# Gate matrices of a product-key expert layer: one float32 product per token in place of three bf16 products, with half of the weighting on ScalarE

## The chip, the cores and the metric

The kernel runs on one core of a Trainium2 chip. The metric is device time in microseconds (us) of one launch, as a median of several runs. TensorE (PE in the rows) multiplies matrices, VectorE (DVE) and ScalarE (ACT) work elementwise, GpSimd (POOL) here splits weights and issues gathers, and SyncE (SP) issues most transfers. PEld is the loading of the stationary operand into TensorE, which overlaps its matmuls.

## The reference

One decoder layer for 528 prompt tokens and 64 sample tokens: norm, one wide input projection, a short gated convolution, a chunked state-space scan, an output projection, and then PEER, a retrieval of single-neuron experts. The change touches PEER alone:

```
s = einsum(q, sub_keys)                       # per head: 2 x 128 scores
s_top, i_top = top_k(s, 16)                   # per half
best_s, best_c = top_k(all 16 x 16 sums, 16)
i1, i2 = the two half keys of each pick       # eid = i1 * 128 + i2
g = softmax(best_s)
act = gelu(u_tab[eid] . t)
out = sum over 8 heads x 16 picks of g * act * v_tab[eid]
```

Each token thus has 128 picks, each of them a pair of keys (i1, i2) with a weight g.

## The kernel before

For 448 of the 576 kept tokens the kernel doesn't gather the experts. It computes the activations of all 16,384 experts densely, multiplies them by a gate that is zero where a token didn't pick the expert, and multiplies by the second table densely too. For the other 128 tokens it gathers rows with indirect DMAs (L603, on POOL), and DVE makes a dot product with each (`row_dot`, L1877).

The dense part runs in 128 units. `activations(m)` on PE (the matmuls of L888) is 24 float32 matmuls of 448 columns, from weights that ACT copies into a rounded high part (`expert_hi`, L1298) and POOL completes with a low part (L611, `w_lo`, two slots). `gelu` (L1321) on ACT reads the result. The first 73 units run beside the search for the picks; `scores(j)` (L901) there is 16 plain float32 matmuls with 128 columns of keys as the moving operand, five sets of them.

Then come the gates, in NB = 28 blocks of TB = 16 tokens. The 128 picks of a token stand on the partitions. For a token, `oh_a` is a 128x128 one-hot matrix (pick x first key) and `oh_w` one of pick x second key times the weight; their product over the picks is the token's gate matrix, exactly as the sum over picks puts it. The operands are bf16. So that the float32 weight isn't rounded it is held as three bf16 pieces (`pickb[:, 2:5]`, made by L1967 to L1969 out of `wrest`), and each token takes three matmuls that add up in PSUM (L937), 48 per block.

- DVE, `one_hots(b, par)`: two comparisons (L1959, L1960) and three multiplications (L1963 twice, L1964), each of 128x2048 bf16, into one of two buffer pairs. It may start when `gates(b - 2)` is done (s_gm) and ends with s_oh.
- PE, `gates(b, par, first)`: waits for s_oh and for the copy of the block before (s_gt), then the matmuls into PSUM banks 4 to 7.
- ACT, `gates_out(b)` (L1363): copies the banks to `gt`, from where SP stores to DRAM.

The order on each engine is written out by hand. PE runs the gates of a block and then `UB[b]` units: one unit in 12 of the 28 blocks, two in the other 16. A block with one unit is called short here. DVE runs the one-hots of block b + 1 and then the dot products of block b (two, or three in every fourth block). After the gates the kernel finishes the units, loads gates and activations back, and runs the second table.

Of the kernel before, what the change touches and what calls it, by code (L numbers as in the profile page):

```python
# [5 lines left out]
ALU = mybir.AluOpType  # L6
ACT = mybir.ActivationFunctionType
# [132 lines left out]
def trunk(nc, xT, x_rows, units, keys, cols, heads, hist_a, hist_s, ssm_in, rows_u, rows_v,  # L140
# [6 lines left out]
    with ExitStack() as ctx:  # L147
        def at(name, off, shape, dt=F32):
            n = 2 if dt is BF16 else 4
# [11 lines left out]
        def stack(start):  # L161

            pos = [start]

            def put(name, shape, dt=F32):
                n = 2 if dt is BF16 else 4
# [9 lines left out]
        ident = const("ident", [P, P])  # L176
        A_CAUSAL = pos[0]
        causal = const("causal", [P, P])
# [121 lines left out]
        mid, mpos = stack(R_MA)  # L300
        pickb = mid("pickb", [P, 5, ND], BF16)
        wrest = mid("wrest", [P, ND])
        iota2 = at("iota2", A_CAUSAL, [P, P, 2], BF16)
        ge = [mid(f"ge{i}", [P, ND]) for i in range(2)]
# [6 lines left out]

        oh_a = at("oh_a", R_XS, [P, 2, TW_, P, 2], BF16)
        oh_w = at("oh_w", R_XS + 4 * TB * P, [P, 2, 3, TW_, P, 2], BF16)
        gt = at("gt", R1, [P, 2, NKEYS, SB])
# [115 lines left out]
        s_eq = sem("one_hots_compared")  # L430
        s_oh = sem("one_hots_ready")
        s_gm = sem("gates_built")
        s_gt = sem("gates_copied")
# [186 lines left out]
        def _(pe):  # L620
# [309 lines left out]
            def gates(b, par, first):  # L930
                pe.wait_ge(s_oh, b + 1)
                if not first:
                    pe.wait_ge(s_gt, b)
                for j in range(TB):
                    a, c = divmod(j, 2)
                    for i in range(3):
                        last = mm(ps[:, 4 + j // 4, j % 4 * P:(j % 4 + 1) * P], oh_a[:, par, a, :, c],  # L937
                                  oh_w[:, par, i, a, :, c], start=i == 0, stop=i == 2)
                last.then_inc(s_gm, 1)
# [45 lines left out]
        def _(act):  # L985
# [353 lines left out]
            for j in range(len(TT)):  # L1339
# [9 lines left out]
                if j:  # L1349
                    act.wait_ge(s_pkT, j)  # L1350
                    n = P if heads == PH else HALF
                    here = slice(TT[j][0], TT[j][0] + n)
                    act.activation(pickb[:, 0:3, here], S0[:, 0:3 * P].rearrange("p (a t) -> p a t", a=3)[:, :, 0:n],
                                   ACT.Copy)
                    act.activation(wrest[:, here], S0[:, 2 * P:2 * P + n], ACT.Copy).then_inc(s_pks, 1)


            def gates_out(b):
                B, part_ = b // 2, b % 2
                act.wait_ge(s_gm, b + 1)  # L1360
                if B >= 2 and part_ == 0:
# [3 lines left out]
                               ACT.Copy).then_inc(s_gt, 1)  # L1365

            activated(M_TOP)
            activated(M_TOP + 1)
            for b in range(NB):
                gates_out(b)  # L1370
                for m in range(M_BLOCK[b], M_BLOCK[b + 1]):
                    activated(m)
# [79 lines left out]
        def _(dve):  # L1452
# [436 lines left out]
            for j, (t0, heads) in enumerate(TT):  # L1889
# [28 lines left out]
                if j == 0:  # L1918
                    dve.tensor_copy(steps[:], iota[:, 0:TOPK])
                    dve.tensor_copy(iota2[:], iota[:].unsqueeze(2).to_broadcast([P, P, 2]))  # L1920
                link(dve.tensor_copy(bself[:, :, 0:np_], bsel[:, :, 0:np_]))
# [28 lines left out]
            def one_hots(b, par):  # L1950
                if b >= 2:
                    dve.wait_ge(s_gm, b - 1)
                t0 = b * TB
                shape = [P, TW_, P, 2]
                across = iota2[:].unsqueeze(1).to_broadcast(shape)
                key_a, key_b, *weight = (pickb[:, i, t0:t0 + TB].rearrange("p (a c) -> p a c", c=2).unsqueeze(2)
                                         .to_broadcast(shape) for i in range(5))
                plain = oh_w[:, par, 2]
                tt_(plain, across, key_b, ALU.is_equal).then_inc(s_eq, 1)  # L1959
                tt_(oh_a[:, par], across, key_a, ALU.is_equal)  # L1960
                dve.wait_ge(s_eq, b + 1)
                for i in range(2):
                    tt_(oh_w[:, par, i], plain, weight[i], ALU.mult)  # L1963
                tt_(plain, plain, weight[2], ALU.mult).then_inc(s_oh, 1)  # L1964

            dve.wait_ge(s_pks, len(TT) - 1)
            link(tt_(wrest[:], wrest[:], pickb[:, 2], ALU.subtract))  # L1967
            link(dve.tensor_copy(pickb[:, 3], wrest[:]))
            link(tt_(pickb[:, 4], wrest[:], pickb[:, 3], ALU.subtract))  # L1969
            one_hots(0, 0)  # L1970
# [160 lines left out]
```

## Time and profile before

| | us |
|---|---|
| median of 3 runs | 2379.86 (2379.05 to 2383.71) |
| the profiled execution | 2379.05 |
| its span, first to last instruction | 2377.1 |
| PE busy in the span | 2344.5 (99%) |
| DVE busy | 1614.3 (68%) |
| POOL busy | 1412.2 (59%) |
| ACT busy | 772.7 (33%) |

The execution's own time is 1.95 us above its span. A matmul in plain float32 with 128 columns leaves two records in the trace, so the 16 matmuls of a set of scores read x32. A row of the timeline gives start, duration, engine, line, operation, output <- inputs, and in brackets how long the engine sat idle before it and who released it. Durations of successive instructions overlap by about a tenth of a us on ACT and DVE and by more on PE, so paces are read from starts.

### The profile page before, as it was taken

The numbers are of one execution on the slowest core, as the hardware profiler recorded it, in microseconds if no ns is written. First come the engines' busy times: TensorE is split into PE (matmuls) and PEld (weight loads), VectorE is DVE, ScalarE is ACT, GpSimd is POOL, SyncE is SP. The second block draws the span as 40 slices with busy tenths as digits, with TensorE's granted clock in tenths as the row PEclk, the third lists the DMA queues.
The fourth block names the chain that finished last, engine by engine and source line by source line (L and its number), as shares of the span: only waits on it lengthen the run. The fifth ranks groups of instructions, "written<-read, shape, count | busy, mean of one in ns | idle before, by whom it ended". The sixth has DMA issues, their size and how long they took to land.

```text
span 2377.1 us, 38840 instructions
## 1 busy us (share of the span) xinstructions
PE 2344.5 (99%) x14998; PEld 2188.6 (92%) x14998; DVE 1614.3 (68%) x2671; ACT 772.7 (33%) x1059; POOL 1412.2 (59%) x787
## 2 busy tenths in 40 slices
PE   9999999999999999999999999999999999999998
PEld 9999999987899999999999989999889999999997
DVE  7865444556775244097987879999577766677774
ACT  4432323332231012233343344444333333333332
POOL 5554334432444555447676757777667777777763
PEclk9999999999999999999999999999999999999999
DMA  5223223236742232247676759999988888888872
GB/s 215 77 80 140 93 99 97 98 108 229 270 171 83 81 128 95 86 134 268 236 261 238 251 169 329 327 329 319 352 302 325 322 315 333 317 319 318 324 269 76
DMA packets 207745, 510.05 MB, mean 215 GB/s; under 512 B 15857, under 2 KB 104305, under 8 KB 205169
## 3 DMA queue, kind: packets, MB, share of 16 engines
q1 hardware_dynamic: 115552, 236.75, 30.9%
q10 hardware_dynamic: 55184, 137.07, 15.5%
q0 software_dynamic: 36864, 134.23, 15.2%
q8 instruction: 100, 1.64, 0.3%
q14 instruction: 45, 0.36, 0.0%
HBM read 424.55 MB, written 83.44 MB: 214 GB/s over the span
## 4 chain that ended last, share of the span: by engine, by line
PE 91%; DVE 5%; DMA 2%; ACT 1%; issue 1%; ACTq 0%; DVEq 0%; SPq 0%; POOL 0%; POOLq 0%
PE ps L888 51%; PE ps L635 30%; PE ps L937 3%; DVE prev L1678 1%; PE ps L901 1%; PE ps L807 1%; PE ps L794 1%; PE ps L802 1%; PE ps L811 1%; DMA gbuf<-gate_scratch 1%; PE ps L827 1%; DMA cxb<-parked_tiles 0%; PE ps L660 0%; PE ps L780 0%; DMA raw<-units 0%
## 5 line engine op out<-in xcount | busy, mean ns | idle before, releaser
L584 POOL TENSOR_SCALAR w_hi<-raw 128x1024 fp32r<-128x1024 f32 x129 | 139.2, 1079 | 521.1 <-issue 391.6
L611 POOL TENSOR_TENSOR w_lo<-raw,e_hi 128x1024 fp32r<-128x1024 f32 x128 | 320.7, 2505 | 176.6 <-PE ps L888 169.1
L611 POOL TENSOR_TENSOR w_lo<-raw,w_hi 128x1024 fp32r<-128x1024 f32 x128 | 315.8, 2468 | 180.7 <-PE ps L888 179.5
L888 PE MATMUL ps<-p_hi,w_lo 128*128 128x448 f32 x1024 | 375.0, 366 | 0.0
L888 PE MATMUL ps<-g_hi,w_lo 128*128 128x448 f32 x1024 | 374.7, 366 | 0.0
L586 POOL TENSOR_TENSOR w_lo<-raw,w_hi 128x1024 fp32r<-128x1024 f32 x129 | 319.1, 2473 | 10.7
L635 PE MATMUL ps<-h_hi,w_hi 128*128 128x296 f32 (+1 forms) x1216 | 273.7, 306 | 1.8 <-ACT ma L1204 1.8
L635 PE MATMUL ps<-h_lo,w_hi 128*128 128x296 f32 (+1 forms) x1216 | 262.5, 297 | 0.0
L635 PE MATMUL ps<-h_hi,w_lo 128*128 128x296 f32 (+1 forms) x1216 | 262.2, 297 | 0.0
L1298 ACT ACTIVATE e_hi<-raw 128x1024 fp32r<-128x1024 f32 x128 | 135.8, 1061 | 263.2 <-DMA raw<-units 126.4
L635 PEld LDWEIGHTS ps<-h_hi,w_hi 128*128 128x128 f32 x1216 | 196.1, 188 | 25.9 <-issue 23.8
L888 PEld LDWEIGHTS ps<-g_hi,w_lo 128*128 128x128 f32 x1024 | 192.2, 188 | 15.1
L888 PEld LDWEIGHTS ps<-p_hi,w_lo 128*128 128x128 f32 x1024 | 192.2, 188 | 15.1
L1298 ACT ACTIVATE w_hi<-raw 128x1024 fp32r<-128x1024 f32 x128 | 135.9, 1062 | 197.4 <-PE ps L888 156.2
L635 PEld LDWEIGHTS ps<-h_lo,w_hi 128*128 128x128 f32 x1216 | 196.2, 188 | 0.0
L635 PEld LDWEIGHTS ps<-h_hi,w_lo 128*128 128x128 f32 x1216 | 196.1, 188 | 0.0
L888 PE MATMUL ps<-g_hi,w_hi 128*128 128x448 f32 x512 | 188.6, 368 | 1.3 <-ACT abuf L1319 1.3
L603 POOL DMA_INDIRECT ug<-rows_u,eid x128 | 170.3, 1331 | 30.8 <-issue 16.7
L888 PE MATMUL ps<-p_hi,e_hi 128*128 128x448 f32 x512 | 186.7, 365 | 1.8 <-DVE p_lo L2006 1.6
L888 PE MATMUL ps<-g_hi,e_hi 128*128 128x448 f32 x512 | 188.2, 368 | 0.2 <-ACT abuf L1319 0.2
L888 PE MATMUL ps<-p_hi,w_hi 128*128 128x448 f32 x512 | 187.2, 366 | 0.2 <-DVEq L1987 0.2
L888 PE MATMUL ps<-p_lo,w_hi 128*128 128x448 f32 x512 | 187.1, 365 | 0.0
(337 smaller groups left out, 5176.9 us busy)
## 6 DMA issues: line engine op xcount, KB each, us to landing
raw<-units SPq DMA_DIRECT2D x385, 512.0 KB
gate_scratch<-gt SPq DMA_DIRECT2D x56, 512.0 KB
activation_scratch<-ge ACTq DMA_DIRECT2D x120, 224.0 KB
abuf<-activation_scratch ACTq DMA_DIRECT2D x30, 896.0 KB, 6.1
gbuf<-gate_scratch ACTq DMA_DIRECT2D x30, 896.0 KB
prev<-ssm_in ACTq DMA_DIRECT2D x8, 1024.0 KB, 7.0
ssm_s<-prev ACTq DMA_DIRECT2D x8, 1024.0 KB, 4.2
parked_tiles<-stage ACTq DMA_DIRECT2D x24, 296.0 KB, 2.1
```

The costliest lines, as they stand in the source:

```text
L584: pool.tensor_scalar(w_hi[:, s, :], raw[:, r, :], 1.0, 1.0, ALU.mult, ALU.mult).then_inc(s_whi, 1)
L586: pool.tensor_tensor(w_lo[:, s, :], raw[:, r, :], w_hi[:, s, :].bitcast(F32), ALU.subtract)\
L603: pool.indirect_dma_start(out=ug[j % UG][:], out_offset=None, in_=table, in_offset=bass.IndirectOffsetOnAxis(ap=eid[:, k:k + 1], axis=0)). ...
L611: pool.tensor_tensor(w_lo[:, n % 2, :], raw[:, n % RAW, :], e_hi[m % HS_].bitcast(F32), ALU.subtract)\
L635: last = mm(a[:, h, :], w, m[:, k0 + k, t0 + h * w_:t0 + (h + 1) * w_], start=start and k == 0 and i == 0, stop=stop and k == KT - 1 and i ...
L794: mm(S1[p0:p0 + HEADDIM, h // 2 * n:(h // 2 + 1) * n], xh, wT[0:n, h, 0:n], start=True, stop=True)
L802: last = mm(S2[j % 2 * n:(j % 2 + 1) * n, :], cmf[:, b * TS:(b + 1) * TS], prev[:, (2 * g + j // 4) % 3, j % 4, :], start=j < 2, stop=j >= ...
L807: last = mm(S2[:, j * n:(j + 1) * n], state[:, g, j * P:(j + 1) * P], Cg, start=True, stop=True)
L811: mm(S3, bT[0:n, :], xde[0:n, :], start=True, stop=True).then_inc(s_st, 1)
L888: last = mm(accp[par], w[:, k * P:(k + 1) * P], x_[:, k, t0:t0 + ND], start=k == 0 and i == 0, stop=k == KT - 1 and i == 2)
L937: last = mm(ps[:, 4 + j // 4, j % 4 * P:(j % 4 + 1) * P], oh_a[:, par, a, :, c], oh_w[:, par, i, a, :, c], start=i == 0, stop=i == 2)
L1298: act.activation(e_hi[m % HS_], raw[:, n % RAW, :], ACT.Copy).then_inc(s_ehi, 1)
```

## The change

The one-hots are float32, and each token takes one plain float32 matmul in place of three bf16 ones. The weight is no longer cut in pieces. It is multiplied into the first-key one-hot, `oh_g`; the second, `oh_2`, stays plain. DVE multiplies the first 8 tokens of a block (`TW_`), and ACT the other 8 in a new helper `weigh`, one activation of 128x128 each with the weight as a scale per partition, in place. PE waits for the new semaphore s_ow besides s_oh. The interleaved copy of the counting row (`iota2`) goes, and `pickb` and `wrest` become one tile `pickT`.

```diff
@@ tiles
-        pickb = mid("pickb", [P, 5, ND], BF16)
-        wrest = mid("wrest", [P, ND])
-        iota2 = at("iota2", A_CAUSAL, [P, P, 2], BF16)
+        pickT = mid("pickT", [P, 3, ND])
-        oh_a = at("oh_a", R_XS, [P, 2, TW_, P, 2], BF16)
-        oh_w = at("oh_w", R_XS + 4 * TB * P, [P, 2, 3, TW_, P, 2], BF16)
+        oh_g = at("oh_g", R_XS, [P, 2, TB, P])
+        oh_2 = at("oh_2", R_XS + 8 * TB * P, [P, 2, TB, P])
@@ PE, gates
                 pe.wait_ge(s_oh, b + 1)
+                pe.wait_ge(s_ow, b + 1)
                 if not first:
                     pe.wait_ge(s_gt, b)
                 for j in range(TB):
-                    a, c = divmod(j, 2)
-                    for i in range(3):
-                        last = mm(ps[:, 4 + j // 4, j % 4 * P:(j % 4 + 1) * P], oh_a[:, par, a, :, c],
-                                  oh_w[:, par, i, a, :, c], start=i == 0, stop=i == 2)
+                    last = mm(ps[:, 4 + j // 4, j % 4 * P:(j % 4 + 1) * P], oh_g[:, par, j, :], oh_2[:, par, j, :],
+                              start=True, stop=True)
@@ ACT
-                    act.activation(pickb[:, 0:3, here], S0[:, 0:3 * P].rearrange("p (a t) -> p a t", a=3)[:, :, 0:n],
-                                   ACT.Copy)
-                    act.activation(wrest[:, here], S0[:, 2 * P:2 * P + n], ACT.Copy).then_inc(s_pks, 1)
+                    act.activation(pickT[:, :, TT[j][0]:TT[j][0] + n],
+                                   S0[:, 0:3 * P].rearrange("p (a t) -> p a t", a=3)[:, :, 0:n],
+                                   ACT.Copy).then_inc(s_pks, 1)
+            def weigh(b):
+
+                act.wait_ge(s_eq, b + 1)
+                for j in range(TW_, TB):
+                    oh = oh_g[:, b % 2, j, :]
+                    t = b * TB + j
+                    last = act.activation(oh, oh, ACT.Copy, scale=pickT[:, 2, t:t + 1])
+                last.then_inc(s_ow, 1)
+
             activated(M_TOP)
+            act.wait_ge(s_pks, len(TT) - 1)
+            weigh(0)
             activated(M_TOP + 1)
             for b in range(NB):
                 gates_out(b)
+                if b + 1 < NB:
+                    weigh(b + 1)
                 for m in range(M_BLOCK[b], M_BLOCK[b + 1]):
                     activated(m)
@@ DVE, one_hots
-                plain = oh_w[:, par, 2]
-                tt_(plain, across, key_b, ALU.is_equal).then_inc(s_eq, 1)
-                tt_(oh_a[:, par], across, key_a, ALU.is_equal)
+                across = iota[:].unsqueeze(1).to_broadcast([P, TB, P])
+                key_a, key_b, weight = (pickT[:, i, t0:t0 + TB].unsqueeze(2).to_broadcast([P, TB, P]) for i in range(3))
+                tt_(oh_g[:, par], across, key_a, ALU.is_equal).then_inc(s_eq, 1)
+                tt_(oh_2[:, par], across, key_b, ALU.is_equal)
                 dve.wait_ge(s_eq, b + 1)
-                for i in range(2):
-                    tt_(oh_w[:, par, i], plain, weight[i], ALU.mult)
-                tt_(plain, plain, weight[2], ALU.mult).then_inc(s_oh, 1)
+                low = oh_g[:, par, 0:TW_]
+                tt_(low, low, weight[:, 0:TW_], ALU.mult).then_inc(s_oh, 1)
             dve.wait_ge(s_pks, len(TT) - 1)
-            link(tt_(wrest[:], wrest[:], pickb[:, 2], ALU.subtract))
-            link(dve.tensor_copy(pickb[:, 3], wrest[:]))
-            link(tt_(pickb[:, 4], wrest[:], pickb[:, 3], ALU.subtract))
             one_hots(0, 0)
```

On PE, at the second block of gates, the kernel before has this row of instructions (acc0_read: the accumulator is free; weights_split: the low part of the weights is there):

```order
L888 MATMUL ps<-g_hi,w_lo 128x448
L937 MATMUL ps<-oh_w,oh_a 128x128 [waits gates_copied,one_hots_ready]
L937 MATMUL ps<-oh_w,oh_a 128x128 x47
L888 MATMUL ps<-g_hi,e_hi_156 128x448 [waits acc0_read,weights_split]
L888 MATMUL ps<-g_lo,e_hi_156 128x448
```

The changed kernel has there (oh_174 is oh_2 under a number of the allocator; its lines are numbered anew):

```order
L886 MATMUL ps<-g_hi,w_lo 128x448
L934 MATMUL ps<-oh_174,oh_g 128x128 [waits gates_copied,one_hots_weighted,one_hots_ready]
L934 MATMUL ps<-oh_174,oh_g 128x128 x15
L886 MATMUL ps<-g_hi,e_hi_163 128x448 [waits acc0_read,weights_split]
L886 MATMUL ps<-g_lo,e_hi_163 128x448
```

The burst stands at the same place, with 16 matmuls for 48, and waits for one more semaphore. On ACT, from the last copy of picks to the gates of the first block, before:

```order
L1353 ACTIVATE pickb<-ps 128x3x64
L1355 ACTIVATE wrest<-ps 128x64
L1321 ACTIVATE ge_164<-ps 128x448
L1323 DMA activation_scratch<-ge_164 128x448
L1298 ACTIVATE e_hi_165<-raw 128x1024
L1321 ACTIVATE ge_163<-ps 128x448
L1323 DMA activation_scratch<-ge_163 128x448
L1298 ACTIVATE w_hi<-raw 128x1024
L1363 ACTIVATE gt<-ps 128x128x16
```

And in the changed kernel:

```order
L1349 ACTIVATE pickT<-ps 128x3x64
L1318 ACTIVATE ge_162<-ps 128x448
L1320 DMA activation_scratch<-ge_162 128x448
L1295 ACTIVATE e_hi_163<-raw 128x1024
L1369 ACTIVATE oh_g<-oh_g,pickT 128x128 x8
L1318 ACTIVATE ge_161<-ps 128x448
L1320 DMA activation_scratch<-ge_161 128x448
L1295 ACTIVATE w_hi<-raw 128x1024
L1359 ACTIVATE gt<-ps 128x128x16
L1369 ACTIVATE oh_g<-oh_g,pickT 128x128 x8
```

Eight activations come between two units ahead of the first gates, and eight behind each copy of gates, ahead of the next unit's gelu.

## Rows read from the trace of the kernel before

**Rows 1.** The page: busy time, share of the span, instructions.
```profile
PE 2344.5 (99%) x14998; PEld 2188.6 (92%) x14998; DVE 1614.3 (68%) x2671; ACT 772.7 (33%) x1059; POOL 1412.2 (59%) x787
```

**Rows 2.** Two windows: length, busy per engine, PEclk, DMA share, GB/s.
```profile
1400.00:1690.00 290.00, 290.00 (x2353) 269.38 (x2352) 273.27 (x257) 121.24 (x115) 207.66 (x102) 1.00 0.94 311
...
1394.50:1397.50 3.00, 2.95 (x29) 2.98 (x30) 3.00 (x3) 0.00 (x0) 0.00 (x0) 0.52 0.44 164
```

**Rows 3.** Chain of waits around the gates: start, us, what.
```profile
1391.12 3.30 DVE oh_w L1964
...
1394.55 4.22 PE ps L937 x48
...
1663.81 4.92 PE ps L888 x24
1668.73 2.77 PE ps L937 x48
1671.50 9.78 PE ps L888 x48
```

**Rows 4.** Waits from 1380 to 1690: total us, times, longest.
```profile
DVE ug L1877 <- DMA ug<-rows_u,eid: 14.9, 13, 4.1
...
ACT gt L1363 <- DMA gate_scratch<-gt: 6.1, 3, 3.0
PE ps L937 <- DVE oh_w L1964: 4.2, 1, 4.2
```

**Rows 5.** Chain of waits at two sets of scores.
```profile
1084.86 3.57 PE ps L901 x32
...
1259.03 3.26 PE ps L901 x32
```

**Rows 6.** Timeline of PE at a set of scores.
```profile
1084.70 3.73 PE L901 MATMUL ps<-key_sb,q 128*128 128x128 f32 x32
1088.18 0.45 PE L888 MATMUL ps<-g_hi,w_hi 128*128 128x448 f32 x1
```

**Rows 7.** Timeline of PE at a block of gates.
```profile
1501.86 2.93 PE L937 MATMUL ps<-oh_w,oh_a 128*128 128x128 bf16 x48
1504.60 0.45 PE L888 MATMUL ps<-g_hi,w_hi 128*128 128x448 f32 x1
```

**Rows 8.** Timeline of ACT: before the first gates, after a later block, and early.
```profile
1386.61 1.06 ACT L1298 ACTIVATE e_hi<-raw 128x1024 fp32r<-128x1024 f32 x1 [0.47 <-ACT ge L1321]
...
1504.83 1.88 ACT L1363 ACTIVATE gt<-ps 128x2048 f32<-128x2048 f32 x1 [0.63 <-PE ps L937]
...
9.80 3.50 ACT L1019 ACTIVATE hu_hi<-x,col 128x592 fp32r<-128x592 f32 x5
```

**Rows 9.** ACT by line and shape: count, busy, mean ns, idle before.
```profile
L1298 ACT ACTIVATE e_hi<-raw 128x1024 fp32r<-128x1024 f32 x128 | 135.8, 1061 | 263.2 <-DMA raw<-units 126.4 <-PE ps L888 102.4 <-ACT ge L1321 26.6
L1394 ACT ACTIVATE p_hi<-abuf 128x448 fp32r<-128x448 f32 x128 | 72.5, 567 | 30.2 <-DVE abuf L2001 23.6 <-issue 6.3
...
L1019 ACT ACTIVATE hu_hi<-x,col 128x592 fp32r<-128x592 f32 x8 | 5.6, 779 | 0.0
```

**Rows 10.** Timeline of DVE: before the first gates, and around block 26.
```profile
1382.53 0.62 DVE L1967 TENSOR_TENSOR wrest<-wrest,pickb 128x448 f32<-128x448 f32 x1 [7.77 <-ACT wrest L1355]
...
1663.83 3.43 DVE L1963 TENSOR_TENSOR oh_w<-oh_w,pickb 128x2048 bf16<-128x2048 bf16 x1
1667.18 1.21 DVE L1964 TENSOR_TENSOR oh_w<-oh_w,pickb 128x2048 bf16<-128x2048 bf16 x1
```

**Rows 11.** One DVE line: ns min/median/max, starts, forms.
```profile
L1650 DVE TENSOR_TENSOR seg<-ps,dqT x20: 682/1225/1226, 236.7 to 589.0; 128x1024 f32<-128x1024 f32 x16, 64x512 f32<-64x512 f32 x4
```

**Rows 12.** POOL by line, 1380 to 1690: count, busy, mean ns, idle before.
```profile
L603 POOL DMA_INDIRECT ug<-rows_u,eid x58 | 97.8, 1686 | 13.6 <-issue 10.4 <-DVE dots L1877 0.5 <-PE ps L888 0.3
L611 POOL TENSOR_TENSOR w_lo<-raw,w_hi 128x1024 fp32r<-128x1024 f32 x24 | 60.8, 2535 | 39.7 <-PE ps L888 39.5
```

**Rows 13.** The gathers' line over the whole span: ns min/median/max, starts.
```profile
L603 POOL DMA_INDIRECT ug<-rows_u,eid x128: 937/962/1972, 1077.9 to 1723.1; - x128
```

More of the change, by code:

```diff
@@ L148, in at @@
         def at(name, off, shape, dt=F32):
-            n = 2 if dt is BF16 else 4
+            n = 4
             for s in shape[1:]:
@@ L165, in put @@
             def put(name, shape, dt=F32):
-                n = 2 if dt is BF16 else 4
+                n = 4
                 for s in shape[1:]:
@@ L176, in trunk @@
         ident = const("ident", [P, P])
-        A_CAUSAL = pos[0]
         causal = const("causal", [P, P])
@@ L431, in trunk @@
         s_oh = sem("one_hots_ready")
+        s_ow = sem("one_hots_weighted")
         s_gm = sem("gates_built")
@@ L1351, in _ @@
                     n = P if heads == PH else HALF
-                    here = slice(TT[j][0], TT[j][0] + n)
-                    act.activation(pickb[:, 0:3, here], S0[:, 0:3 * P].rearrange("p (a t) -> p a t", a=3)[:, :, 0:n],
-                                   ACT.Copy)
-                    act.activation(wrest[:, here], S0[:, 2 * P:2 * P + n], ACT.Copy).then_inc(s_pks, 1)
+                    act.activation(pickT[:, :, TT[j][0]:TT[j][0] + n],
+                                   S0[:, 0:3 * P].rearrange("p (a t) -> p a t", a=3)[:, :, 0:n],
+                                   ACT.Copy).then_inc(s_pks, 1)
             def gates_out(b):
@@ L1919, in _ @@
                     dve.tensor_copy(steps[:], iota[:, 0:TOPK])
-                    dve.tensor_copy(iota2[:], iota[:].unsqueeze(2).to_broadcast([P, P, 2]))
                 link(dve.tensor_copy(bself[:, :, 0:np_], bsel[:, :, 0:np_]))
@@ L1953, in one_hots @@
                 t0 = b * TB
[L1954 to L1957, printed above, removed]
-                plain = oh_w[:, par, 2]
-                tt_(plain, across, key_b, ALU.is_equal).then_inc(s_eq, 1)
-                tt_(oh_a[:, par], across, key_a, ALU.is_equal)
+                across = iota[:].unsqueeze(1).to_broadcast([P, TB, P])
+                key_a, key_b, weight = (pickT[:, i, t0:t0 + TB].unsqueeze(2).to_broadcast([P, TB, P]) for i in range(3))
+                tt_(oh_g[:, par], across, key_a, ALU.is_equal).then_inc(s_eq, 1)
+                tt_(oh_2[:, par], across, key_b, ALU.is_equal)
                 dve.wait_ge(s_eq, b + 1)
-                for i in range(2):
-                    tt_(oh_w[:, par, i], plain, weight[i], ALU.mult)
-                tt_(plain, plain, weight[2], ALU.mult).then_inc(s_oh, 1)
+                low = oh_g[:, par, 0:TW_]
+                tt_(low, low, weight[:, 0:TW_], ALU.mult).then_inc(s_oh, 1)
             dve.wait_ge(s_pks, len(TT) - 1)
-            link(tt_(wrest[:], wrest[:], pickb[:, 2], ALU.subtract))
-            link(dve.tensor_copy(pickb[:, 3], wrest[:]))
-            link(tt_(pickb[:, 4], wrest[:], pickb[:, 3], ALU.subtract))
             one_hots(0, 0)
```

## The prediction

> **What bounds the kernel now.** I read the page's busy times first, then the windows of the gate stage, the chain of waits through it, the table of waits, and last the timelines of single engines. PE is busy for 99% of the span [rows 1]. In the stage that the change touches, 1400 to 1690 us, it is busy for all 290 us at the full clock, while DVE is busy for 273 of them (94%), POOL for 208 and ACT for 121 [rows 2]. The chain there is PE alone: a burst of gates of 2.77 us, 4.92 us for one unit or 9.78 us for two, and so on [rows 3]. So each us that a burst grows is a us on the end, as long as nobody else is late. Two things are to be seen besides. PE waits in this stage in earnest just once: 4.2 us for DVE's last one-hot before the first burst [rows 4]. And that first burst takes 4.22 us instead of 2.77 [rows 3]; the granted clock in its first 3 us is 0.52 [rows 2], the lower of the two levels (1.2 instead of 2.4 GHz), which it fell to behind that wait. And DVE, though off the chain, has little to spare: in block 26, a short one, its last product ends at 1668.39 (1667.18 + 1.21 [rows 10]) and the burst starts at 1668.73 [rows 3], 0.34 us later.
>
> **The burst on PE.** Removed per block: 48 bf16 matmuls. Added: 16 plain float32 matmuls of 128x128 by 128 columns. That is exactly a set of scores, L901: same shape, same banks, each followed by a unit. Its price is in the trace twice over. By the chain, 3.57 us [rows 5] against 2.77 [rows 3], 0.80 more. From starts, burst to first unit matmul behind it: 1088.18 - 1084.70 = 3.48 us [rows 6] against 1504.60 - 1501.86 = 2.74 [rows 7], 0.74 more. The one set with 64 tokens (half the stationary width) takes 3.26 [rows 5], 0.49 more; I keep that as the low end although its shape differs. With 28 blocks: 28 x 0.74 = 20.7, 28 x 0.80 = 22.4, low end 28 x 0.49 = 13.7. I take 21.0, near the count from starts, since starts are recorded and ends modelled. A third as many matmul instructions is thus not a third of the time: a float32 matmul costs 3.48/16 = 218 ns and a bf16 one 2.74/48 = 57 ns, so one replaces three of 171 ns in all. Nothing hides the difference, PE being the chain.
>
> **The first block.** Three vector operations (L1967 to L1969) go, and the one-hots can begin at 1382.5, where L1967 starts now [rows 10]. PE would have been ready at 1394.55 - 4.2 = 1390.35 [rows 3, 4]. DVE: float32 products took 625 ns for 448 columns (0.62 [rows 10]) and 1225 ns for 1024 [rows 11], so 1.04 ns a column, and 2.29 us for 2048, 1.22 for the 1024 of the multiplication; spaced 0.1 closer each, 5.5 us in all, ending at 1388.0, or at 1390.3 if POOL's split (2.5 us [rows 12]) holds up one of them as in block 26, where a product of 1.21 took 3.43 [rows 10], 2.2 us more. ACT: it ends e_hi at 1386.61 + 1.06 = 1387.67 [rows 8] and then weighs. Price of one weighing: no activation of 128 columns with a scale per partition stands in the rows. From 1061 ns for 1024 columns and 567 for 448 a column costs 0.86 ns; the one with such a scale has 779 ns for 592 [rows 9], so 779 - 464 x 0.86 = 380 ns for 128. Five in a row of those took 3.50 us [rows 8], (3.50 - 0.78)/4 = 0.68 apart, 0.1 closer than their duration. So 0.28 us each, between 0.2 (a further tenth of overlap) and 0.38 (none). I take 0.28, by the row that has the same kind of scale: 2.24 us, ending at 1389.9; at 0.38, 1390.7. All three arrive at about 1390.3. The wait of 4.2 us goes but for some tenths, and the clock doesn't fall, so the burst gives back 4.22 - 2.77 = 1.45 too: 5.65, of which I count 5.4.
>
> **The later blocks, ACT.** The new wait of PE is for ACT. What is queued behind the weighing there is the next gelu, the next store and e_hi; gelu frees the accumulator for the unit after next, at least 4.9 us on. The tight case is a short block. The copy starts at 1504.83 and takes 1.88 [rows 8], the weighing 2.24, so it ends at 1508.95. PE's next burst would start at 1504.60 + 4.92 + 0.2 = 1509.7. The slack of 0.76 us is used up at 0.375 us each, so even the high end loses 0.04 us in each of 12 blocks, 0.5 in all. Copies that wait for stores (3, 6.1 us in all [rows 4]) come, by their starts, ahead of two-unit stretches, where twice the slack is there. I count nothing.
>
> **The later blocks, DVE.** Five products of 1.21 us spaced 1.13 apart, 5.65 us, become 2.2 + 2.2 + 1.1 = 5.5. The wait for the first comparison is met one instruction later. ACT needs the first comparison only, which comes 2.2 us after the start; the bounds for DVE are a gain of 0.15 us a block and one more stoppage by POOL, a loss of 2.2. Since each block of PE grows by 0.75 us and DVE's work doesn't, its slack should grow from block to block. Counted at nothing. Had it no slack left, a us of DVE in a short block would be a us of the end.
>
> **POOL.** A gather takes 0.96 us as a median over the span with a maximum of 1.97 [rows 13], but 1.69 as a mean in this stage [rows 12], where DVE runs products out of two SBUF tiles for half of the time. It ends up waiting for the DVE instruction under way. That instruction now lasts 2.3 us and not 1.2, so a gather may take up to 1.1 us more, and so may a split. POOL has 290 - 208 = 82 us idle [rows 2]; if each of the 58 gathers and twice 24 splits [rows 12] lost 0.55 us, 58 us would go, and it still keeps up. The Trainium skill, page SBUF — State Buffer, section Who interferes with whom, says that a vector instruction with two SBUF inputs contends with GpSimd instructions that read SBUF and not with those that only write, whoever issued first holding the port to the end. For the splits the trace agrees (3.43 for 1.21 [rows 10]); by that rule the gathers, which write descriptors, would be free of it, and their 1.69 against 0.96 speaks against that part. The sum by either is the same as long as POOL keeps up.
>
> **The sum.** 2379.05 + 21.0 - 5.4 = 2394.65 us for the execution profiled; that one is 0.8 below the median of the three. I say 2395.
>
> **The rivals.**
> 1. *A wait takes the place of the one removed.* DVE or POOL falls behind in short blocks: the stage has DVE at 94% [rows 2], slack of 0.34 us at block 26, and DVE already waits 14.9 us for gathered rows [rows 4]; with gathers held longer, rows land later, dot products come later, one-hots behind them too. Against it: PE's stage grows by 21 us and DVE's own work doesn't. If PE waits 1 us in each of the 12 short blocks, 2394.7 + 12 = 2407; at 2 us, 2419.
> 2. *The other side: faster.* The two records of a float32 matmul might run as one pass here, the one-hots being contiguous: 16 x 0.109 = 1.74 us a burst, 28 x (1.74 - 2.77) = -28.8, and 2345 with the 5.4. The place is the burst, and it decides below 2.74/16 = 171 ns a matmul, or below 183 with the first wait counted in (5.4/28/16 = 12 ns more). For it: one instruction in place of three. Against it: five sets of scores, out of contiguous tiles too, at 204 to 223 ns.
> 3. *Cheaper bursts.* At the low end of 0.49 us: 2379.05 + 13.7 - 5.4 = 2387.4. For it only the narrow set of scores.
> 4. *The first wait stays.* If ACT's eight activations or DVE's last product come 2 us late, 2 of the 4.2 stay and the clock may fall again: 2394.7 + 3.5 = 2398. It lies inside the range.
>
> **Chances.** Forecast with rival 4: 0.74, 2391 to 2400. Rival 1: 0.17. Rival 3: 0.05. Rival 2: 0.04. The range of 2388 to 2406 leaves out rival 2, most of rival 3's low part and the larger half of rival 1. A measurement of this kernel can tell 0.2% (4.8 us) from no change. Slower by more than that (from 2384.7 on): forecast, rival 1 and most of rival 3, 0.93. Within it: 0.03, from rival 3 and a milder rival 2. Faster: 0.04.
>
> **What would show it.** Per burst two records for each of 16 matmuls, and 3.5 to 3.6 us of the chain; the first burst near 1390.4 with no fall of the clock; no wait of PE for ACT's weighing or for DVE beyond some tenths; the eight weighings in 2.0 to 2.6 us; DVE comparisons of 2.3 us, some of 4.5; gathers up to 3 us long. The forecast is wrong if a burst takes less than 3.2 us, or if the table of waits has PE behind DVE, ACT or POOL in the short blocks with more than 5 us in all.

## The result, and the profile after

The changed kernel takes 2410.5 us as a median of 4 runs (2405.44 to 2411.7; seven further executions on record lie between 2407.87 and 2416.41), the kernel before beside it 2381.38 (2379.05 to 2383.71): a ratio of 1.0127, with a 95% interval of 1.0111 to 1.0142. It is slower, as forecast, but by 29 us and not by 16, and 2410.5 lies above the range. The profiled execution took 2407.87 us with a span of 2406.0, 28.9 above the span of before.

The busy times of the page, to be read beside [rows 1]:

```profile
PE 2380.0 (99%) x14550; PEld 2214.3 (92%) x14550; DVE 1607.6 (67%) x2611; ACT 837.2 (35%) x1279; POOL 1432.2 (60%) x787
```

The chain of waits of the changed kernel from 1383 on, which answers to [rows 3] (a burst is the row of matmuls that makes a block's gates, L934; L886 are the units):

```profile
1383.24 10.06 PE ps L886 x48
1393.30 3.62 PE ps L934 x32
1396.92 9.77 PE ps L886 x48
...
1423.70 4.87 PE ps L886 x24
1428.57 3.57 PE ps L934 x32
...
1700.27 3.57 PE ps L934 x32
1703.85 14.65 PE ps L886 x72
```

A burst is 3.57 us, to the hundredth what a set of scores costs [rows 5], and the first one 3.62, with no wait ahead of it. The timeline around the burst at 1428, to be read beside [rows 6, 7]: 1431.89 - 1428.40 = 3.49 us from start to start.

```profile
1428.40 3.73 PE L934 MATMUL ps<-oh,oh_g 128*128 128x128 f32 x32
1431.89 0.45 PE L886 MATMUL ps<-g_hi,e_hi 128*128 128x448 f32 x1
```

PE's own waits, over the whole span, the three longest. None is for a one-hot or a weighing, where [rows 4] has 4.2 us:

```profile
PE ps L706 <- POOL rowmask L573: 3.6, 1, 3.6
PE ps L825 <- DVE xs L1707: 2.7, 4, 0.7
PE ps L633 <- DVE hu_lo L1516: 2.0, 2, 1.6
```

With that the stage of the gates can be summed. From the start of the first burst to the end of the last it lasts 1703.85 - 1393.30 = 310.55 us, where the chain of before gives 1684.04 - 1394.55 = 289.49:

```profile
1681.28 2.77 PE ps L937 x48
1684.04 6.14 PE ps L888 x30
```

That is 21.06 more, 28 bursts against 28 bursts. But the ends lie further apart. Here is the whole account, from the chains and from the start of the first dense unit (1008.08 before, 1006.88 after):

| stretch | before | after | difference |
|---|---|---|---|
| to the first dense unit | 1008.08 | 1006.88 | -1.2 |
| dense units until PE is ready for the first burst | 382.27 | 386.42 | +4.15 |
| wait for the one-hots | 4.20 | 0 | -4.2 |
| first burst to end of last burst | 289.49 | 310.55 | +21.06 |
| from there to the end of the span | 693.06 | 702.15 | +9.1 |
| span | 2377.1 | 2406.0 | +28.9 |

Two stretches grew, 4.15 and 9.1 us, in which no matmul was changed, and one of them lies ahead of the first burst. What they have in common is the dense unit. In the same 300 us of the second table, so many of its matmuls start; the first row is the kernel before, the second the changed one (two separate answers, with the length, PE's busy time and count, the clock, DMA share and GB/s):

```profile
1960.00:2260.00 300.00, 299.91 (x1480) 1.00 0.88 322
```

```profile
1960.00:2260.00 300.00, 300.00 (x1460) 1.00 0.87 317
```

1480 against 1460, 202.7 ns against 205.5, at full clock and with PE busy throughout. The matmuls of the projections before 1003 us kept their pace (2896 start between 200 and 600 us in both kernels). 6144 matmuls of a dense unit stand in the span, so 2 to 3 ns on each is the whole of what the sum lacked (28.9 - 15.6 = 13.3 us, or 2.2 ns each).

### The profile page after: what moved, and what is told of

Its sections match the earlier page's. It is cut to its first block, busy times and chain, and to the rows that moved or that the text cites. A ratio compares the mean times of both kernels' runs of the same rounds, so it can differ in the third digit from the quotient of the medians.

```text
span 2406.0 us, 38105 instructions
## 1 busy us (share of the span) xinstructions
PE 2380.0 (99%) x14550; PEld 2214.3 (92%) x14550; DVE 1607.6 (67%) x2611; ACT 837.2 (35%) x1279; POOL 1432.2 (60%) x787
## 4 chain that ended last, share of the span: by engine, by line
PE 91%; DVE 5%; DMA 2%; ACT 1%; issue 1%; DVEq 0%; SPq 0%; ACTq 0%
PE ps L886 52%; PE ps L633 29%; PE ps L934 4%; DMA cxb<-parked_tiles 1%; DVE prev L1687 1%; PE ps L899 1%; PE ps L805 1%; PE ps L792 1%; PE ps L800 1%; PE ps L809 1%; PE ps L825 1%; PE ps L658 0%; DMA gbuf<-gate_scratch 0%; PE ps L778 0%; DVE hu_lo L1516 0%
## 5 line engine op out<-in xcount | busy, mean ns | idle before, releaser
L609 POOL TENSOR_TENSOR w_lo<-raw,w_hi 128x1024 fp32r<-128x1024 f32 x128 | 324.3, 2534 | 188.3 <-PE ps L886 187.5
L886 PE MATMUL ps<-p_hi,w_lo 128*128 128x448 f32 x1024 | 376.2, 367 | 0.0
L886 PE MATMUL ps<-g_hi,w_lo 128*128 128x448 f32 x1024 | 375.6, 367 | 0.0
L584 POOL TENSOR_TENSOR w_lo<-raw,w_hi 128x1024 fp32r<-128x1024 f32 x129 | 318.5, 2469 | 10.8
L886 PEld LDWEIGHTS ps<-p_hi,w_lo 128*128 128x128 f32 x1024 | 192.2, 188 | 18.2
L886 PEld LDWEIGHTS ps<-g_hi,w_lo 128*128 128x128 f32 x1024 | 192.2, 188 | 17.5
L1886 DVE CUSTOM_DVE_ANT_0 ug<-ug,ps 128x1024 f32<-128x1024 f32 x128 | 153.7, 1213 | 78.3 <-DMA ug<-rows_u,eid 78.0
L601 POOL DMA_INDIRECT ug<-rows_u,eid x128 | 179.2, 1400 | 29.2 <-issue 17.9
L1986 DVE TENSOR_TENSOR x<-x,ps 128x448 f32<-128x448 f32 x128 | 79.5, 621 | 167.8 <-PE ps L886 164.6
L886 PE MATMUL ps<-g_hi,w_hi 128*128 128x448 f32 x512 | 189.5, 370 | 1.4 <-ACT abuf L1316 1.4
L886 PE MATMUL ps<-p_hi,e_hi 128*128 128x448 f32 x512 | 187.5, 366 | 1.7 <-DVE p_lo L2007 1.6
L886 PE MATMUL ps<-g_hi,e_hi 128*128 128x448 f32 x512 | 188.9, 369 | 0.0
```

What stands on the lines that cost most here:

```text
L584: pool.tensor_tensor(w_lo[:, s, :], raw[:, r, :], w_hi[:, s, :].bitcast(F32), ALU.subtract)\
L601: pool.indirect_dma_start(out=ug[j % UG][:], out_offset=None, in_=table, in_offset=bass.IndirectOffsetOnAxis(ap=eid[:, k:k + 1], axis=0)). ...
L609: pool.tensor_tensor(w_lo[:, n % 2, :], raw[:, n % RAW, :], e_hi[m % HS_].bitcast(F32), ALU.subtract)\
L886: last = mm(accp[par], w[:, k * P:(k + 1) * P], x_[:, k, t0:t0 + ND], start=k == 0 and i == 0, stop=k == KT - 1 and i == 2)
L1886: dve.tensor_tensor_reduce(rows, rows, h_rows, 1.0, 0.0, ALU.mult, ALU.add, dots[:, k:k + 1])\
L1986: tt_(xu, xu, accp[p_], ALU.add).then_inc(s_x2, 1)
```

## The experiments

Every time is a median beside runs of the kernel before on the same chip; that kernel's own median was 2382.03, 2382.6, 2381.44 and 2384.0 in the four groups of runs.

**Where the units' pace comes from.** The change also altered a placement: `pickT` is 896 bytes smaller than `pickb` and `wrest` together, and all tiles behind it in that stack moved down by that: the gelu buffers `ge`, `e_hi1` (one of the four slots of the weights' high part; e_hi0, w_hi[1] and w_hi[0] are the others), `eid` and a buffer for gathered rows. The first two runs exchange the placements.

```diff
+++ e1_layout_of_before (on the changed kernel)
         pickT = mid("pickT", [P, 3, ND])
+        mid("pad", [P, 224])
```

> The changed kernel with an unused tile of 896 bytes behind pickT, so that the tiles behind it (the two gelu buffers ge, e_hi1, eid, the last gathered-row buffer) stand at the addresses that they have in the kernel before. Theory P (place): the pace of the dense units, 205.5 ns a matmul in the changed kernel's second-table stage against 202.8 before, comes from where e_hi1 or the gelu buffers stand; then it returns to about 202.8, and the time to 2410.5 - 14 = 2396 (2393 to 2399), which is the sum of the prediction. Rival S (a state that doesn't hang on places, such as one that differs from one build or load to the next): the pace stays at 205 to 206 and the time within 3 us of 2410.

2397.41 us (2397.24 to 2399.57), ratio 1.0062 (1.0038 to 1.0086), and 1480 matmuls in the 300 us again:

```profile
1960.00:2260.00 300.00, 299.91 (x1480) 1.00 0.89 320
```

Its chain around the first burst, and from the last burst on:

```profile
1384.03 9.87 PE ps L887 x48
1393.90 0.00 issue
1393.90 3.81 PE ps L935 x32
...
1699.71 3.57 PE ps L935 x32
1703.28 14.65 PE ps L887 x72
```

Summed like the table above (first dense unit at 1011.69, span 2395.3), e1 has 382.21 us until the first burst, with no wait, 309.38 in the stage of the gates and 692.02 behind it. The two stretches outside the gates are back to what the kernel before has (382.27 and 693.06). In the stage e1 is 19.89 us above the kernel before, so 1.2 of the 21.06 us were the units' pace too. The span is 3.6 us longer for a reason that has nothing to do with the change: the first dense unit starts later. Over the 17 traces it starts anywhere between 1006.9 and 1014.6 us, so an account by stages says more than the spans of two single executions do.

```diff
+++ e2_before_moved (on the kernel before)
-        wrest = mid("wrest", [P, ND])
+        mid("pad", [P, 224])
-        eid = mid("eid", [P, N_PICK], U32)
+        eid = at("eid", A_CAUSAL + 512, [P, N_PICK], U32)
         ug = [...] + [mid(f"ug{UG - 1}", [P, D])]
+        wrest = mid("wrest", [P, ND])
```

> The kernel before with ge and e_hi1 moved 896 bytes down, to the addresses of the changed kernel (wrest goes behind them, eid onto constants no longer used, the last row buffer ends up 1408 bytes lower). Bf16 gates as before. Theory P: the pace of the dense units goes from 202.8 to about 205.5 ns, 6144 matmuls by 2.5 ns, so 2381 + 14 = 2395 (2391 to 2399). Rival S: 2381 within 3 us.

2395.86 us (2394.67 to 2399.94), ratio 1.0052 (1.0033 to 1.007), and the pace of the changed kernel under the instructions of before:

```profile
1960.00:2260.00 300.00, 300.00 (x1460) 1.00 0.88 316
```

Theory P holds both ways; S is out. Then which tile:

```diff
+++ e5_e_hi1_up (on the changed kernel)
+        mid("pad", [P, 224])
         e_hi1 = mid("e_hi1", [P, D], F32R)
+++ e6_behind_e_hi1 (on the changed kernel)
         e_hi1 = mid("e_hi1", [P, D], F32R)
+        mid("pad", [P, 224])
```

> The changed kernel with 896 unused bytes ahead of e_hi1: the gelu buffers stay where the change put them, and e_hi1, eid and the last row buffer stand as in the kernel before. Theory W (it is the place of the weights): the pace in the second-table stage goes from 205.7 to 202.8 ns, 487 matmuls in 100 us become 494, and the time is 2396. Rival G (the gelu buffers' place): 487 in 100 us and 2410.

> The changed kernel with the 896 unused bytes behind e_hi1: gelu buffers and e_hi1 as the change put them, eid and the last row buffer as before. Theory W: 487 matmuls in 100 us and 2410, as in the changed kernel. Rival R (the place of the gathered rows' buffer, which DMAs write): 494 and 2396.

e5: 2399.22 (2396.89 to 2399.98). e6: 2413.01 (two runs, 2407.41 and 2418.61). The windows, e5 first:

```profile
1960.00:2260.00 300.00, 299.91 (x1480) 1.00 0.88 321
```

```profile
1960.00:2260.00 300.00, 300.00 (x1460) 1.00 0.87 316
```

Neither the gelu buffers nor the row buffer matters to the pace. It is the place of e_hi1, a tile that the change doesn't name.

```diff
+++ e7_e_hi1_by_32 (on the changed kernel)
+        mid("pad", [P, 8])
         e_hi1 = mid("e_hi1", [P, D], F32R)
+++ e8_both_by_32 (as e7, and)
+        late("pad0", [P, 8])
         e_hi0 = late("e_hi0", [P, D], F32R)
```

> The changed kernel with 32 unused bytes ahead of e_hi1, which then starts at a multiple of 64 bytes, like the slots in w_hi and unlike e_hi0 (odd multiples of 32 in both kernels). Theory A (the alignment to 64 bytes sets the pace of a slot): units out of e_hi1 run at the pace that units of w_hi have, and the time moves from 2410 to between 2396 and 2405. Rival F (finer or coarser places count, not the multiple of 64): e_hi1's units stay at about 205 ns, 2410.

> The changed kernel with both e_hi0 and e_hi1 moved 32 bytes up, so that all four slots of the high parts start at multiples of 64 bytes. Theory A: one pace for all units, at the 202.8 of w_hi before (2396) or at the 206.7 that w_hi has in the changed kernel (about 2420). Rival F: as in the run with e_hi1 alone.

e7: 2402.79 (2399.46 to 2404.73). e8: 2397.36 (2393.09 to 2404.68). Both moved the time, so 32 bytes suffice, but neither theory had all of it. The pace in the second table, from the starts of successive matmuls within a unit, by the slot of its high part (ns a matmul). The residue is that of the slot's offset from the start of the kernel's own tiles; that start is itself at 128 modulo 256 in the partition, so the addresses in the partition have residues 128 further on. The expectations count as the table does:

| kernel | e_hi0 (mod 256) | e_hi1 (mod 256) | w_hi[1] (64) | w_hi[0] (64) |
|---|---|---|---|---|
| before | 204.3 (224) | 200.6 (160) | 202.9 | 203.1 |
| changed | 204.1 (224) | 204.9 (32) | 206.7 | 206.7 |
| e2 | 204.1 (224) | 204.9 (32) | 206.7 | 206.7 |
| e1, e5 | 204.3 (224) | 200.6 (160) | 202.8 | 202.9 |
| e7 | 204.4 (224) | 202.8 (64) | 202.8 | 202.6 |
| e8 | 201.1 (0) | 204.3 (64) | 204.2 | 204.1 |
| e9 | 201.3 (0) | 200.7 (160) | 202.9 | 203.1 |
| e14 | 201.2 (0) | 200.5 (160) | 202.8 | 202.9 |
| e15 | 204.0 (224) | 204.3 (224) | 202.8 | 202.8 |

Units out of w_hi, which never moved, run at 202.9 or 206.7 according to where e_hi1 is. The slots take turns in this order, so e_hi1's place reaches the two units behind it and not e_hi0's, which comes third (204.3 and 204.1). By what route it does is not shown; all slots share the low parts `w_lo` and the moving operand, and no run moved those.

```diff
+++ e9_before_e_hi0_up (on the kernel before)
+        late("pad0", [P, 8])
         e_hi0 = late("e_hi0", [P, D], F32R)
```

> The kernel before with e_hi0 32 bytes up (a multiple of 64), nothing else. In the run with both moved, units out of e_hi0 took 201.1 ns a matmul and not 204.3. If that belongs to e_hi0's own place, 1536 of the 6144 matmuls gain 3.2 ns: 5 us, 2377 against 2382, and 494 matmuls in 100 us become 497. Rival: the pace of a slot hangs on the pair of places and carries over into the next units; then the units of e_hi1 or w_hi lose what e_hi0 gains, 2382 or up to 2390.

2378.41 (2376.73 to 2383.14, 10 runs) against 2381.44: ratio 0.999 with an interval of 0.9978 to 1.0002, so the time alone doesn't settle it. The pace does: e_hi0's units 204.3 to 201.3, the others as before, and 1485 matmuls in the window.

```profile
1960.00:2260.00 300.00, 299.88 (x1485) 1.00 0.89 322
```

```diff
+++ e14_changed_both_places (on e5)
+        late("pad0", [P, 8])
         e_hi0 = late("e_hi0", [P, D], F32R)
+++ e15_before_e_hi1_by_64 (on the kernel before)
+        mid("pad", [P, 16])
         e_hi1 = mid("e_hi1", [P, D], F32R)
```

> The changed kernel with e_hi1 at its place of before (896 bytes up; 2399.2 alone) and e_hi0 32 bytes up. Theory: places act one by one, e_hi0's units at 201.3 and e_hi1's at 200.6 as in the kernel before with the same places; 2392 to 2395. Rival: in the changed kernel with e_hi1 32 bytes up, e_hi0's move slowed the three other slots by 1.4 ns each, and it does so here.

> The kernel before with e_hi1 64 bytes up, which puts it at 224 modulo 256, where e_hi0 stands in the kernel before (204.3 ns), instead of 160 (200.6). Theory M (the place modulo 256 sets a slot's own pace): e_hi1's units go to about 204.3 and the time to 2387 or more. Rival N: they stay at 200.6 to 201 and 2381, so that the place modulo 256 doesn't tell the pace.

e14: 2399.62 (2394.79 to 2404.81) where 2392 to 2395 was expected. The paces are those of the theory (201.2, 200.5, and w_hi untouched), and the median doesn't show it. The execution traced is the slowest of the three, and PE waits longer in it for the low part of the second table's moving operand, `p_lo`. The first row is e5, the second e14:

```profile
PE ps L887 <- DVE p_lo L2008: 1.6, 1, 1.6
```

```profile
PE ps L888 <- DVE p_lo L2009: 8.6, 3, 3.8
```

Eight of the 17 traces have such a further wait of 3.0 to 3.9 us (e14 has two), with and without the change, so part of the scatter of the times is likely this and not the place of a tile. What makes DVE late there stays open. e15: 2387.81 (2385.97 to 2392.8), ratio 1.0023 (1.0005 to 1.004), and e_hi1 at 204.3: theory M called it. Rival N is out for this place. The residue of 64 has given 202.8 and 204.3 though (e_hi1 in e7 and e8), so the residue modulo 256 alone doesn't tell a pace, and what the hardware does there stays open.

**What a burst is worth.**

```diff
+++ e3_two_pieces (on the kernel before)
-                    for i in range(3):
+                    for i in range(2):
                         ... start=i == 0, stop=i == 1)
```

> The kernel before with two of the three bf16 pieces of the weight multiplied in: 32 matmuls a block instead of 48 (the lowest piece of the weight is left out of the gates). All else, DVE's five products too, unchanged. Theory: a burst is on the path with its whole length, at 57 ns a matmul, so it takes 2.77 - 16 x 0.057 = 1.86 us in the chain and the time falls by 28 x 0.91 = 25 us to 2356; the pace of the units stays at 202.8. Rival: DVE, busy for 94% of the stage and with 0.3 us of slack in short blocks, becomes late as PE gets ahead; PE then waits for L1964 in the short blocks, and less than 15 of the 25 us come through (over 2366).

2384.41 (2375.21 to 2391.27, 8 runs), ratio 1.0006 (0.9988 to 1.0024): nothing came through, and the rival was right. The chain and the waits of that kernel:

```profile
1409.84 1.85 PE ps L937 x32
...
1423.27 4.92 PE ps L888 x24
1428.33 3.01 POOL w_lo L611
1431.49 8.09 DMA ug<-rows_u,eid
1439.60 1.22 DVE ug L1877
```

```profile
PE ps L937 <- DVE oh_w L1964: 24.7, 7, 5.1
```

The burst did fall to 1.85, as expected, and the chain leaves PE: it runs over POOL, the gather and DVE, and PE waits 24.7 us for the one-hots. The waits cost more than their length: behind the five of 4.0 us and more the burst took 2.7 to 3.4 us from its start to the next unit's, where the others took 1.8. The clock shows why, here behind the wait of 5.1 us:

```profile
1505.84:1508.84 3.00, 3.00 (x30) 3.00 (x31) 3.00 (x5) 0.00 (x0) 0.88 (x1) 0.52 0.96 307
```

The stage of before has two bounds that nearly touch. Then DVE's load was cut with PE's:

```diff
+++ e12_two_pieces_four_products (on e3)
-                plain = oh_w[:, par, 2]
+                plain = oh_w[:, par, 1]
-                for i in range(2):
-                    tt_(oh_w[:, par, i], plain, weight[i], ALU.mult)
-                tt_(plain, plain, weight[2], ALU.mult).then_inc(s_oh, 1)
+                tt_(oh_w[:, par, 0], plain, weight[0], ALU.mult)
+                tt_(plain, plain, weight[1], ALU.mult).then_inc(s_oh, 1)
-            link(tt_(pickb[:, 4], wrest[:], pickb[:, 3], ALU.subtract))
```

> The kernel before with two of the three bf16 pieces (the lowest is left out of the gates), and now DVE's third product for it left out too. With 32 matmuls and five products the bursts fell to 1.85 us, 25 us less, and nothing of it came through: PE waited 24.7 us for DVE. Theory: a shorter burst is worth its length only as far as DVE keeps up; with four products (1.1 us less in each of 28 blocks) the wait is mostly gone and 20 to 25 us come through: 2357 to 2362. Rival: something else holds the stage (gathered rows, POOL), 2375 or more.

2353.9 (2353.17 to 2359.88), ratio 0.9892 (0.9873 to 0.991). 27.5 us came through, above the expected 20 to 25. What was left out of the expectation is the first burst: with a product less, DVE is on time there too, the wait of 4.2 us shrinks to 0.2 and the clock stays up. What is left of PE's waits for the one-hots is 1.2 us in four waits, the longest 0.4. This version beats both kernels. With the better place for e_hi0 on top:

```diff
+++ e13_two_pieces_e_hi0_up (on e12)
+        late("pad0", [P, 8])
         e_hi0 = late("e_hi0", [P, D], F32R)
```

> The kernel before with two bf16 pieces, four products on DVE, and e_hi0 32 bytes up. Two pieces alone gave 2353.9; the move alone brought e_hi0's units from 204.3 to 201.3 ns a matmul, 1536 by 3 ns. Theory: the two add up, 2349. Rival: the pace gained at a place doesn't outlast another order of instructions, 2354.

2348.05 (2343.86 to 2357.79), ratio 0.986 (0.9828 to 0.9893); the paces are 201.1, 200.5, 202.8 and 202.9. The two gains add up, as far as a median of four with this scatter can tell. It is the fastest kernel tried, 36 us below the kernel before beside it and 62 below the changed one's own median. Both versions leave out the third piece, so their gates carry the weight to two bf16 pieces and not three.

**The first burst's wait.**

```diff
+++ e4_late_first (on the changed kernel)
+                if b == 0:
+                    for _ in range(2):
+                        link(tt_(oh_2[:, par], across, key_b, ALU.is_equal))
                 tt_(oh_g[:, par], across, key_a, ALU.is_equal).then_inc(s_eq, 1)
```

> The changed kernel with two more comparisons of 2.3 us ahead of the first block's on DVE (they write oh_2, which is then written anew), so that the first burst comes late again. Theory (the first-block term of the sum): DVE ends about 4.5 us later, PE waits some 4 to 4.6 us, the clock falls to the lower level for about 3 us and the first burst takes some 1.5 to 2.5 us more; 5.5 to 7 us more than the changed kernel in the stage. Rival: the clock stays up after a wait of that length, and only the wait itself is lost, 4 to 4.6.

2421.99 (two runs, 2421.02 and 2422.96) against 2410.5. Its wait, its first burst, and the clock in the first 3 us of it:

```profile
PE ps L934 <- DVE oh_g L1971: 6.5, 1, 6.5
```

```profile
1399.77 6.05 PE ps L934 x32
```

```profile
1399.77:1402.77 3.00, 3.00 (x14) 3.00 (x15) 3.00 (x2) 0.00 (x0) 0.00 (x0) 0.50 0.16 62
```

The wait came out at 6.5 us, not 4.5, since two of the comparisons took 4.4 us each beside POOL, and the product behind them was 2.2 us shorter. Behind it the clock is at the lower level (1.2 GHz) and the burst takes 6.05 instead of 3.62, 2.4 us more. 6.5 + 2.4 = 8.9 us against 5.5 to 7 expected (3.0 more of the 11.5 us is one of the waits for p_lo named above); the mechanism is the expected one, and the rival (the clock stays up) is out. In the changed kernel, without the wait, the same window reads 1.00.

```profile
1393.30:1396.30 3.00, 3.00 (x29) 3.00 (x28) 3.00 (x2) 1.60 (x2) 2.85 (x1) 1.00 0.58 225
```

**Who has slack beside the burst.** Both of these stand on e1, whose time is 2397.41.

```diff
+++ e10_act_weighs_12
-                for j in range(TW_, TB):
+                for j in range(TB - 12, TB):
-                low = oh_g[:, par, 0:TW_]
-                tt_(low, low, weight[:, 0:TW_], ALU.mult).then_inc(s_oh, 1)
+                low = oh_g[:, par, 0:TB - 12]
+                tt_(low, low, weight[:, 0:TB - 12], ALU.mult).then_inc(s_oh, 1)
+++ e11_dve_weighs_all
-                tt_(low, low, weight[:, 0:TW_], ALU.mult).then_inc(s_oh, 1)
+                tt_(oh_g[:, par], oh_g[:, par], weight, ALU.mult).then_inc(s_oh, 1)
                 (and weigh, its calls and PE's wait for s_ow removed)
```

> The changed kernel with the layout of before (2397.4), ACT weighing 12 of a block's 16 tokens and DVE 4. ACT's eight weighings take 2.44 us and end 0.4 to 0.5 us ahead of the burst in each of the 12 short blocks. Theory (the estimate of slack): four more at 0.29 us each are 1.17, so PE waits 0.7 us for ACT in each short block, 8 to 9 us in all, 2406. Rival: ACT's wait is taken up elsewhere (the next block's wait is shorter by as much), 2397.

2414.41 (two runs, 2412.87 and 2415.96). The chain, at a short block, and the waits:

```profile
1423.69 4.87 PE ps L887 x24
1428.56 0.65 issue
1429.21 3.81 PE ps L935 x32
```

```profile
PE ps L935 <- issue: 7.2, 11, 0.7
PE ps L887 <- DVE p_lo L2008: 5.5, 2, 3.9
```

PE waits about 0.65 us behind 11 short blocks, 7.2 in all, and the chain gives the bursts there 3.81 instead of 3.57, 2.6 more. Most of that isn't a slower burst. The chain counts a piece from the modelled end of the piece before it, and only behind a gap from its own start; so e1's first burst reads 3.81 too, with a gap of 0.00. From start to start a burst takes 3.57 us behind such a wait and 3.49 elsewhere. Together it is 9.8 of 17, and the stage grew by 9.9 over e1's. One of the further waits for p_lo, 3.9 us, stands at 1881 us, well inside the second table, and is another part. The wait is put down to "issue" although it is ACT's weighing that ends then (the twelve run from 1425.51 for 3.60 us); DVE had been done for 9 us.

> The changed kernel with the layout of before (2397.4) and all 16 tokens weighted on DVE (products of 2048, 2048 and 2048), ACT's part and its semaphore gone. DVE's one-hots end at least 1.1 us ahead of the burst in all blocks but two (0.1 in the first, 0.6 in block 26). Theory: DVE takes that, apart from the first block; 2398 to 2400. Rival: DVE, with 1.1 us more in each of 28 blocks, falls behind in the short ones and PE waits over 5 us for it, 2405 or more.

2404.35 (two runs, 2403.67 and 2405.04), 7 us over e1, between theory and rival. PE waits for DVE three times, 5.1 us in all, the first burst among them:

```profile
PE ps L934 <- DVE oh_g L1964: 5.1, 3, 2.2
```

Behind the longest of them, 2.2 us, the clock is down to 0.62, and the burst takes 5.22 us from start to start, 1.7 more:

```profile
1633.77:1636.77 3.00, 3.00 (x17) 3.00 (x18) 3.00 (x5) 0.00 (x0) 2.85 (x2) 0.62 0.84 279
```

So half of the weighting on ACT is worth about 7 us to the float32 version, and four tokens more cost 10 in the stage alone.

## Why the prediction was right or wrong

**The burst: right.** 28 x 0.75 = 21.0 and another 1.45 off for the first one's clock, net 19.6; measured 21.06 from first burst to last end, and 19.89 with the placement of before (e1). The two ways of pricing it had given 0.74 and 0.80. The chain's 0.80 seems to fit the 21.06 (27 x 0.80 - 0.60 = 21.0), but that is a coincidence with the slower units: without them the price from starts is the one that comes out (3.49 - 2.74 = 0.75 for each of 27, and 0.5 less than before for the first, 19.8 in all). The term is off by 0.3 us.

**The first block: right.** The wait is gone, 4.2 us, and the clock stays up. PE, ACT and DVE all arrive 2.7 us later than the 1390.3 of the prediction, PE because of the slower units ahead of it and the others with it. Eight weighings took 2.44 us (2.24 predicted):

```profile
1390.42 2.44 ACT L1369 ACTIVATE oh_g<-oh_g,pickT 128x128 f32<-128x128 f32 x8
...
1398.74 2.43 ACT L1369 ACTIVATE oh_g<-oh_g,pickT 128x128 f32<-128x128 f32 x8
```

A weighing has 391 ns as a mean where 380 was worked out from the line with a scale of its own, and they follow each other by 0.29, for 0.28. DVE's last product took 3.43 us beside POOL, as in the high case:

```profile
1385.17 2.29 DVE L1964 TENSOR_TENSOR oh_g<-iota,pickT 128x2048 f32<-128x2048 f32 x1 [7.75 <-ACT pickT L1349]
1387.38 2.29 DVE L1965 TENSOR_TENSOR oh<-iota,pickT 128x2048 f32<-128x2048 f32 x1
1389.58 3.43 DVE L1968 TENSOR_TENSOR oh_g<-oh_g,pickT 128x1024 f32<-128x1024 f32 x1
```

It ends at 1393.01, 0.1 us ahead of the burst.

**ACT and DVE later: right, and how near is now known.** In short blocks ACT ends 0.4 to 0.5 us ahead of the burst (0.76 predicted), and e10 uses it up. DVE's least slack after the first block went from 0.2 to 1.4 us, since PE's blocks grew and its own work did not.

**POOL: right in kind.** The gathers got longer, up to 2.97 us where [rows 13] has 1.97, and POOL kept up. Two of them behind a split of POOL's, and the two DVE instructions beside them:

```profile
1450.54 2.37 POOL L609 TENSOR_TENSOR w_lo<-raw,e_hi 128x1024 fp32r<-128x1024 f32 x1 [2.90 <-PE ps L886]
1453.05 2.84 POOL L601 DMA_INDIRECT ug<-rows_u,eid  x1
1456.19 1.88 POOL L601 DMA_INDIRECT ug<-rows_u,eid  x1 [0.30 <-issue]
```

```profile
1450.93 4.13 DVE L1964 TENSOR_TENSOR oh_g<-iota,pickT 128x2048 f32<-128x2048 f32 x1
1454.98 2.28 DVE L1965 TENSOR_TENSOR oh<-iota,pickT 128x2048 f32<-128x2048 f32 x1
```

The DVE instructions end at 1455.06 and 1457.26, the gathers at 1455.89 and 1458.07, each 0.8 us later, and the shortest gathers take 0.94. So a gather waits for the DVE instruction under way, as the prediction had it, and then runs.

The Trainium skill, page SBUF — State Buffer, section Who interferes with whom, has a vector instruction with two SBUF inputs contend with GpSimd instructions that read SBUF, and reports a probe in which `tensor_tensor` stalled no DMA, inferring as the reason that making descriptors needs the write interface, which such an instruction leaves free. This trace goes against that for the gathers: the gathers' longest time grew by 1.0 us as DVE's instructions beside them grew by 1.1. A gather also reads its row numbers `eid` from SBUF, so the rule on readers may still be the one that holds here; no run separates the two.

**What failed: the sum was taken to be complete.** The failed step is a term put at nothing without a reason. "2379.05 + 21.0 - 5.4" has no term for the 6144 unit matmuls, which are 52% of the chain of the changed kernel. I took their pace as given because their instructions don't change. The diff showed that the tiles ahead of e_hi1 changed in size, and with it where e_hi1 lies, and I didn't follow it. No rival had it either. Measured in its place: 2410.5 - 2397.4 = 13 us with the placement alone put back (e1), 14 us with the placement alone put on the kernel before (e2, 2395.86 against 2382.03), and 4.15 + 9.1 us in the two stretches outside the gates, which the units fill for the most part. Why the pace hangs on the place stays open. The change without its side effect costs 2397.41 - 2382.03 = 15.4 us, ratio 1.0062 (1.0038 to 1.0086), where the sum had 15.6; by stages it is 19.89 - 4.26 = 15.6, the second being the way from the first unit to the first burst. So near a hit is in part luck, since the interval leaves 9 to 20 us open.

**The rivals.** Rival 1 gives 2407 and 2419, and the measured time stands between them, but it is not what happened: in the stage of the gates no wait of PE for DVE or ACT is in the trace. Its mechanism is real nonetheless, one step away on either side (e3, e10, e11). Rivals 2 and 3 fell with the 3.57 us. Rival 4 did not come about either. Its price of 3.5 us for 2 us of lateness is borne out by e11, where a wait of 2.2 us lengthened the burst by 1.7; e4, with 6.5 us, cost 8.9.

## What to carry to other kernels

A change of a tile's size moves every tile behind it. Where one of those feeds the engine that is the chain, compare the pace of its unchanged instructions (matmuls started in a window of equal length) before looking for waits, and pad the tile to its old size to split the change in two. A burst on the chain is worth its length only as far as the next engine keeps up; read that engine's least slack, and cut both loads together. In this kernel three bf16 products of 128 columns (171 ns) cost PE less than one of plain float32 (218 ns).

## What the runs showed of the hardware

The pace of back-to-back float32 (rounded) matmuls of 448 columns, each with its own 128x128 weights, hangs on where the weights start within a partition. In the second table it was between 200.5 and 206.7 ns, at the full clock in all cases, and 32 bytes moved it (e7, e8, e9). With residues counted as in the table, weights that started at 0 or 160 had 200.5 to 201.3 ns in every kernel, 224 had 204.0 to 204.4, 32 had 204.9, and 64 had 202.6 to 206.7, depending on where the other slots lay. The pace of slots that were not moved changed with that of e_hi1 (202.9 to 206.7 ns). Why is open; no run here separates the reading of weights from that of the moving operand.

After a wait of 4.2 us the granted clock was 0.52 in the next 3 us, after one of 6.5 us 0.50, after one of 5.1 us 0.52 (e3) and after one of 2.2 us 0.62 (e11), so that the clock was at its lower level for most of that time. After one of 1.8 us (e11) and after waits of 0.65 us (e10) it read 1.00:

```profile
1694.24:1697.24 3.00, 3.00 (x26) 3.00 (x27) 3.00 (x5) 0.37 (x1) 2.85 (x2) 1.00 1.00 335
```

An indirect gather took 0.94 us at the shortest and up to 2.97 beside float32 products on DVE; in the rows above it ended 0.8 us after the DVE instruction under way.
